# First feed-forward block fed with inputs that are not yet normalised

## The chip, the core and the metric

The kernel runs on one core of a Trainium2 chip. The metric is the device time of one launch in microseconds (us); lower is better. The engines are named as in the profile: PE is TensorE's matmul, PEld its weight load, DVE is VectorE, ACT is ScalarE, POOL is GpSimd, SP is SyncE, whose queue loads the weights.

## What is computed

Two transformer-like blocks on 256 tokens of 1024 features, in float32. The change touches the first feed-forward network (FFN) alone, the very first thing that the kernel does:

```python
def rms_norm(x, g):
    y = xf * lax.rsqrt(jnp.mean(xf * xf, axis=-1, keepdims=True) + RMS_EPS)
    return (y * g.astype(jnp.float32)).astype(x.dtype)

def swiglu(h, w1, w3, w2):
    return (jax.nn.silu(h @ w1) * (h @ w3)) @ w2

x = x + 0.5 * swiglu(rms_norm(x, ffn1_norm[l]), ffn1_w1[l], ffn1_w3[l], ffn1_w2[l])
```

D_MODEL is 1024, D_FF is 2816. The factor r = rsqrt(mean(x^2) + eps) is one number per token; the weight g is one number per feature.

## The kernel before

Activations lie with features on the 128 partitions and the 256 tokens along the free dimension, so x is eight tiles XC[:, 0, k] of 128x256. A norm is: eight squares on ACT into NT (L1544); five adds of squares (k = 1 to 5 into NT[:, 0]) on DVE (L2050, semaphore norm_acc); three sums over partitions on PE, for NT[:, 6], NT[:, 7] and NT[:, 0] (`norm_sum`, L540); the root on ACT (STD, L1548); the reciprocal on DVE (RSTD, L2069); and `norm_spread` (L558), two matmuls that lay r out as a 128x256 tile in PSUM. `norm_rows` then scales the rows on DVE into NT (L2053), rounds them on ACT to H_HI (L1554) and takes the rest H_LO = NT - H_HI on DVE (L2061).

Every float32 product is made of three rounded ones: W_HI x H_HI, W_LO x H_HI and W_HI x H_LO. Weights come in a stream of 1 MB units of 128x2048, through three buffers RAW. For each unit ACT rounds it (`split_hi`, L418, semaphore hi_done) and DVE takes the rest (`split_lo`, L430, semaphore lo_done). The SP queue loads a buffer again once lo_done says that its last unit is split. Unit 0 alone is treated by hand: ACT rounds it in two halves (L1615, L1616), and POOL takes both halves' rest (L499); after that POOL issues the loads of the tables (L501 to L504).

The FFN has 22 tiles t of 128 hidden features. `up(t)` is one unit on PE, which holds the gate tile (w = 0) and the up tile (w = 1): 16 matmuls of 128x512 (L655) and 16 of 128x256 (L659), into PSUM banks 2(t%2) and 2(t%2)+1. `down(i)` is one unit of 48 matmuls of 128x256 on the hidden tiles 2i and 2i+1 (L436, L437, L684). PE's order is written out: up(0), up(1), up(2), down(0), up(3), then a loop of up, down, up, then up(20), down(9), up(21), down(10). `up(t)` waits for lo_done of its unit and, from t = 2 on, for hid_prod of tile t-2, which frees its banks; `down(i)` waits for hid_lo of tile 2i+1.

`hidden(t)` is what stands between them. ACT copies the low halves of the two banks (L1571, L1574); DVE adds the gate (`gate_sum`, L2109); ACT takes silu (L1576); DVE adds the up tile (L2122), multiplies (L2134, hid_prod), rounds (L2139) and takes the rest (L2141, hid_lo). For the last tile, 21, the up tile is read from PSUM (L2127, L2128, L2131). On DVE the calls stand in this order: unit 1's and unit 2's split, hidden(0), unit 3's split, hidden(1), two splits, hidden(2), a split, and so on; at the end gate_sum(21), the split of the next stage's first unit, then the rest of hidden(21). On ACT: unit 2's split, silu(0), unit 3's split, silu(1), and so on. Ahead of unit 2's split ACT loads the table of silu and uses it once, on SCZ (L1621).

## Time and profile before

| | us |
|---|---|
| median of 3 runs | 1649.91 |
| lowest, highest | 1647.41, 1651.48 |
| profiled execution, its time | 1648.0 |
| profiled execution, its span | 1646.2 |
| PE busy in the span | 1627.7 |
| DVE busy | 1115.4 |
| ACT busy | 698.3 |
| POOL busy | 23.9 |

The span runs from the first to the last instruction; all starts below are counted from its beginning. PE is busy for 99% of it, but not in its first 20 us. A row of the timeline is: start, duration, engine, line, operation, output and input, shape, count, and in brackets the idle time ahead of it and who ended it. A duration of back-to-back instructions overlaps the next one's, so the distance between two starts is the price in a row of them.

### The profile page before, as it was taken

Reading aid. Unit: us, or ns where it says so; the run is one execution under the profiler, and the core shown is the slowest. Engines: PE = TensorE matmul, PEld = TensorE weight load, DVE = VectorE, ACT = ScalarE, POOL = GpSimd, SP = SyncE. Lnnn points to the kernel's source line nnn. Section 1 sums busy time; section 2 is a strip of 40 time slices with the busy share of each in tenths; the row PEclk is TensorE's granted clock in tenths of the full one; section 3 lists DMA queues with packets and bytes.
Section 4 is the critical chain, followed back from the end, with each engine's and each line's share of the span. In section 5 each row is a group of like instructions: output and inputs, shape, how many; then the busy total and the mean of one; then the engine's idle time right before and its main releaser. Section 6 shows DMA issues by size and latency. Waiting matters only on the chain.

```text
span 1646.2 us, 30278 instructions
## 1 busy us (share of the span) xinstructions
PE 1627.7 (99%) x12552; PEld 1477.9 (90%) x12552; DVE 1115.4 (68%) x1617; ACT 698.3 (42%) x918; POOL 23.9 (1%) x41
## 2 busy tenths in 40 slices
PE   9999999999999999999999999999999999999998
PEld 7999888899999999988888887988999999999997
DVE  7666657564887766668887874967457676676665
ACT  6444456434455444421222122516354445454443
POOL 1000000000000000000000000000000000000000
PEclk9999999999999999999999999999999999999998
DMA  7555477322265545243456542233323355545551
GB/s 292 178 188 194 154 283 265 120 79 105 104 237 180 203 178 195 98 158 140 164 193 253 193 166 77 103 128 104 108 77 112 146 183 187 194 154 189 192 180 52
DMA packets 37837, 267.80 MB, mean 163 GB/s; under 512 B 4268, under 2 KB 4524, under 8 KB 5744
## 3 DMA queue, kind: packets, MB, share of 16 engines
q1 hardware_dynamic: 33552, 238.25, 40.5%
q0 software_dynamic: 4192, 28.19, 4.5%
q8 instruction: 72, 1.18, 0.3%
q14 instruction: 21, 0.17, 0.0%
HBM read 265.38 MB, written 1.05 MB: 162 GB/s over the span
## 4 chain that ended last, share of the span: by engine, by line
PE 73%; issue 23%; DVE 3%; ACT 1%; DMA 0%; POOL 0%; POOLq 0%; SPq 0%; DVEq 0%; ACTq 0%
PE PS L436 15%; PE PS L437 15%; PE PS L442 11%; PE PS L655 9%; PE PS L828 6%; PE PS L659 5%; PE PS L684 2%; PE PS L892 1%; DVE W_LO L430 1%; PE PS L540 1%; PE PS L872 1%; PE PS L874 1%; PE PS L873 1%; PE PS L1178 0%; PE PS L1353 0%
## 5 line engine op out<-in xcount | busy, mean ns | idle before, releaser
L430 DVE TENSOR_TENSOR W_LO<-RAW,W_HI 128x2048 fp32r<-128x2048 f32 x210 | 476.2, 2269 | 181.8 <-ACT W_HI L418 180.9
L418 ACT ACTIVATE W_HI<-RAW 128x2048 fp32r<-128x2048 f32 x208 | 397.6, 1913 | 362.1 <-PE PS L442 239.9
L436 PE MATMUL PS<-HS,W_HI 128*128 128x256 f32 (+1 forms) x792 | 265.3, 339 | 1.5 <-ACT G L1732 0.8
L437 PE MATMUL PS<-HS,W_LO 128*128 128x256 f32 (+1 forms) x792 | 261.5, 334 | 0.0
L655 PE MATMUL PS<-HS,W_HI 128*128 128x512 f32 x984 | 246.5, 392 | 0.7 <-DVE W_LO L430 0.7
L442 PE MATMUL PS<-HS,W_HI 128*128 128x512 f32 (+1 forms) x712 | 242.1, 340 | 0.0
L436 PE MATMUL PS<-HID_HI,W_HI 128*128 128x256 f32 (+1 forms) x720 | 220.6, 307 | 0.3 <-DVE XC L2598 0.3
L437 PE MATMUL PS<-HID_HI,W_LO 128*128 128x256 f32 (+1 forms) x720 | 220.2, 307 | 0.0
L655 PEld LDWEIGHTS PS<-HS,W_HI 128*128 128x128 f32 x984 | 177.0, 189 | 32.6 <-DVE W_LO L430 0.9
L436 PEld LDWEIGHTS PS<-HS,W_HI 128*128 128x128 f32 x792 | 150.1, 189 | 19.7 <-issue 3.3
L437 PEld LDWEIGHTS PS<-HS,W_LO 128*128 128x128 f32 x792 | 150.2, 190 | 14.9
L442 PEld LDWEIGHTS PS<-HS,W_HI 128*128 128x128 f32 x712 | 134.8, 189 | 15.0
L684 PE MATMUL PS<-HID_LO,W_HI 128*128 128x256 f32 x528 | 147.9, 283 | 0.0
L436 PEld LDWEIGHTS PS<-HID_HI,W_HI 128*128 128x128 f32 x720 | 137.5, 191 | 7.6 <-issue 0.8
L437 PEld LDWEIGHTS PS<-HID_HI,W_LO 128*128 128x128 f32 x720 | 137.5, 191 | 6.2
L659 PEld LDWEIGHTS PS<-HS,W_LO 128*128 128x128 f32 x984 | 134.2, 190 | 9.6
L659 PE MATMUL PS<-HS,W_LO 128*128 128x256 f32 x984 | 137.2, 282 | 0.0
L2152 DVE SCALAR_TENSOR_TENSOR XC<-PS,GATE,XC 128x256 f32<-128x256 f32 x160 | 68.2, 478 | 53.5 <-PE PS L442 53.3
L684 PEld LDWEIGHTS PS<-HID_LO,W_HI 128*128 128x128 f32 x528 | 100.7, 192 | 0.0
L828 PE MATMUL PS<-HS,W_HI 128*128 128x256 f32 x672 | 90.9, 285 | 0.3 <-DVE W_LO L430 0.3
L828 PEld LDWEIGHTS PS<-HS,W_HI 128*128 128x128 f32 x672 | 84.5, 192 | 5.4 <-issue 4.8
L2097 DVE SCALAR_TENSOR_TENSOR SUMS<-LATE,SCZ,SUMS 128x1024 f32<-128x1024 f32 x56 | 70.1, 1282 | 1.4
(442 smaller groups left out, 2425.6 us busy)
## 6 DMA issues: line engine op xcount, KB each, us to landing
RAW<-stream SPq DMA_DIRECT2D x225, 1024.0 KB, 4.8
LATE<-stream POOLq DMA_DIRECT2D x24, 1024.0 KB, 5.1
XC<-xin SPq DMA_DIRECT2D x2, 512.0 KB, 4.6
XC<-xin POOLq DMA_DIRECT2D x1, 1024.0 KB, 5.1
out<-NT SPq DMA_DIRECT2D x4, 256.0 KB, 2.6
CON<-consts POOLq DMA_DIRECT2D x1, 616.0 KB, 6.5
LW<-lora POOLq DMA_DIRECT2D x1, 512.0 KB, 6.7
DFT<-dft POOLq DMA_DIRECT2D x1, 266.0 KB, 2.9
```

The costliest lines, as they stand in the source:

```text
L418: nc.scalar.activation(W_HI[s % RING][:], RAW[PLACE[u]][:], ACT.Copy).then_inc(hi_done, 1)
L430: last = nc.vector.tensor_tensor(W_LO[s % RING][:, o], RAW[PLACE[u]][:, o], W_HI[s % RING][:, o].bitcast(F32), ALU.subtract)
L436: nc.tensor.matmul(acc, w_hi, x_hi, start=first, stop=False)
L437: return nc.tensor.matmul(acc, w_lo, x_hi, start=False, stop=last)
L442: return nc.tensor.matmul(acc, w_hi, x_lo, start=False, stop=last)
L540: last = nc.tensor.matmul(sums(name), tmp[:, k, tt * P:(tt + 1) * P], SQW[:, k, 2 - 2 * tt:6 - 2 * tt] if w == 4 else ONE3[:, 1 - tt:3 - t ...
L655: nc.tensor.matmul(BK8[2 * (t % 2) + w][:].rearrange("p (a n) -> p a n", a=2), W_HI[sl][:, c:c + P], HS[:, :, 0, k], start=(k == 0), stop= ...
L659: last = nc.tensor.matmul(tile(w), W_LO[sl][:, c:c + P], H_HI[:, 0, k], start=False, stop=(k == KT - 1))
L684: return nc.tensor.matmul(acc, W_HI[sl][:, c:c + P], HID_LO[:, t, 0:ROWS], start=False, stop=ends)
L828: last = nc.tensor.matmul(acc, wt[sl][:, c:c + P], x(k), start=(wt is W_HI and x is rhs_hi and k == 0), stop=(x is rhs_lo and k == kt - 1))
L2097: ins = V.scalar_tensor_tensor(out=SUMS[a][:], in0=w, scalar=SCZ[:, z:z + 1], in1=SUMS[a][:], op0=ALU.mult, op1=ALU.add)
L2152: last = V.scalar_tensor_tensor(out=XC[:, h, m], in0=BK8[4 + m % 4][:, h * ROWS:(h + 1) * ROWS], scalar=gate(h, m), in1=XC[:, h, m], op0=A ...
```

## The change

In the first FFN alone, the rows that go into PE are XC times the norm's weight n1, without the factor r. Since r is one factor per token, it commutes with the product over features, and is applied afterwards: to the summed gate tile (ahead of silu) and to the summed up tile, each by one more DVE multiply with RSF, an SBUF copy of the spread factor, which ACT makes. For tile 21 the gate's second multiply takes place on the silu tile, since the up tile stays in PSUM. The norm's own chain (squares, sums, root, reciprocal, spread) is still there, but beside the first matmuls. POOL adds the squares in place of DVE, and DVE takes the rest of unit 0 in place of POOL. In up(0), PE goes through the gate tile's half of the unit as soon as ACT has rounded it, then the other half, then W_HI x H_LO, and W_LO x H_HI last.

```diff
@@ gpsimd
-            pool.wait_ge(landed[0], 16)
-            for h in range(2):
-                pool.wait_ge((S("hi_half"), hi_done)[h], 1)
-                o = slice(h * UNIT // 2, (h + 1) * UNIT // 2)
-                last = nc.gpsimd.tensor_tensor(W_LO[0][:, o], RAW[0][:, o], W_HI[0][:, o].bitcast(F32), ALU.subtract)
-            last.then_inc(lo_done, 1)
+            for k in range(1, NORM_ADDS["na"] + 1):
+                pool.wait_ge(S("norm_sq"), k + 1)
+                if k > 1:
+                    pool.wait_ge(S("norm_acc"), k - 1)
+                nc.gpsimd.tensor_tensor(NT[:, 0], NT[:, 0], NT[:, k], ALU.add).then_inc(S("norm_acc"), 1)
+            pool.wait_ge(landed[PLACE[2]], 16)
@@ tensor, up
-                    if t == 0 and f == 0:
-                        pe.wait_ge(hi_done, 1)
+                    if t < 2 and f == 0:
+                        pe.wait_ge(hi_done if t else S("half"), t + 1)
...
+                        for w in range(2):
+                            if w:
+                                pe.wait_ge(hi_done, 1)
+                            for k in range(KT):
+                                pe.wait_ge(S("norm_hi"), k + 1)
                                 c = (w * KT + k) * P
                                 nc.tensor.matmul(tile(w), W_HI[sl][:, c:c + P], H_HI[:, 0, k], start=(k == 0), stop=False)
+                            if w == 0:
+                                norm_sum("na", 0, first=6, last_k=0)
                         for w in range(2):
                             for k in range(KT):
+                                pe.wait_ge(S("norm_h"), k + 1)
                                 c = (w * KT + k) * P
+                                nc.tensor.matmul(tile_lo(w), W_HI[sl][:, c:c + P], H_LO[:, 0, k], start=False, stop=False)
+                        norm_spread("na")
+                        for w in range(2):
+                            pe.wait_ge(lo_done if w else S("half"), 1 if w else 2)
+                            for k in range(KT):
+                                c = (w * KT + k) * P
+                                last = nc.tensor.matmul(tile(w), W_LO[sl][:, c:c + P], H_HI[:, 0, k], start=False, stop=(k == KT - 1))
+                            last.then_inc(psum_ready, 1)
+                        return
...
+                            if t == 1 and f == 0 and w == 0:
+                                wait_unit(s)
@@ tensor, start
-            for k in (6, 7, 0):
+            pe.wait_ge(S("con_in"), 16)
+            keep_clock(2, 0)
+            for k in (6, 7):
                 norm_sum("na", k, first=6, last_k=0)
-            pe.wait_ge(S("con_in"), 16)
-            keep_clock(1, 0)
-            norm_spread("na")
             keep_clock(2, 0)
@@ scalar, start
+            act.wait_ge(landed[PLACE[0]], 16)
+            A(W_HI[0][:, 0:UNIT // 2], RAW[PLACE[0]][:, 0:UNIT // 2], ACT.Copy).then_inc(S("half"), 1)
+            A(W_HI[0][:, UNIT // 2:], RAW[PLACE[0]][:, UNIT // 2:], ACT.Copy).then_inc(hi_done, 1)
             act.wait_ge(S("par_in"), 16)
             root("na")
...
-            for k in range(KT):
-                round_rows("na", 0, k)
             split_hi(act, 1)
+            act.wait_ge(S("norm_spread"), NORM["na"] + 1)
+            A(RSF[:], spread_of("na"), ACT.Copy).then_inc(S("row_scale"), 1)
@@ vector, ffn
+                def by_rms(ins, rows_, n_, j=None, j0=0):
+
+                    ins.then_inc(S("summed"), 1)
+                    dve.wait_ge(S("row_scale"), 1)
+                    dve.wait_ge(S("summed"), n_ if j is None else (j - j0) * 4 + n_)
+                    return V.tensor_tensor(rows_, rows_, RSF[:], ALU.mult)
...
                     if t == FT - 1:
+                        if f == 0:
+                            link(V.tensor_tensor(SILU[:, 1, 0:ROWS], SILU[:, 1, 0:ROWS], RSF[:], ALU.mult))
@@ vector, start
-            for k in range(1, 6):
-                add_squares("na", k)
             dve.wait_ge(S("par_in"), 16)
-            dve.wait_ge(S("con_in"), 16)
+            for k in range(KT):
+                dve.wait_ge(S(f"x_in{k // 4}"), 16)
+                V.tensor_scalar(H_HI[:, 0, k], XC[:, 0, k], par("n1", k), None, ALU.mult).then_inc(S("norm_hi"), 1)
+            for k in range(KT):
+                dve.wait_ge(S("norm_hi"), k + 1)
+                V.scalar_tensor_tensor(out=H_LO[:, 0, k], in0=XC[:, 0, k], scalar=par("n1", k), in1=H_HI[:, 0, k].bitcast(F32),
+                                       op0=ALU.mult, op1=ALU.subtract).then_inc(S("norm_h"), 1)
             reciprocal("na")
-            norm_rows("na", 0, lambda k: par("n1", k))
-            dve.wait_ge(lo_done, 1)
+            for h in range(2):
+                dve.wait_ge(hi_done if h else S("half"), 1)
+                o = slice(h * UNIT // 2, (h + 1) * UNIT // 2)
+                V.tensor_tensor(W_LO[0][:, o], RAW[PLACE[0]][:, o], W_HI[0][:, o].bitcast(F32), ALU.subtract).then_inc(lo_done if h else S("half"), 1)
             split_lo(dve, 1)
```

The other lines of the diff only renumber semaphore counts (norm_t, row_scale).

PE from its first matmul to up(1), before. PS<-WARM and PS<-CON keep the engine at work, PS<-ONE_81,NT are the sums of squares, PS<-CON,RSTD the spread; W_HI_52 and W_LO_55 are unit 0, W_HI_53 and W_LO_56 unit 1.

```order
1 L901 MATMUL PS<-WARM 128x256 x9
2 L540 MATMUL PS<-ONE_81,NT 128x2 x6
3 L552 MATMUL PS<-CON 128x256
4 L558 MATMUL PS<-CON,RSTD 128x128 x2
5 L552 MATMUL PS<-CON 128x256 x2
6 L630 MATMUL PS<-HS,W_HI_52 128x256 x16
7 L635 MATMUL PS<-HS,W_LO_55 128x256 x16
8 L647 MATMUL PS<-HS,W_HI_52 128x256 x16
9 L655 MATMUL PS<-HS,W_HI_53 128x512 x8
```

And the same stretch of PE now:

```order
1 L915 MATMUL PS<-WARM 128x256 x9
2 L552 MATMUL PS<-CON 128x256 x2
3 L540 MATMUL PS<-ONE_81,NT 128x2 x4
4 L552 MATMUL PS<-CON 128x256 x2
5 L632 MATMUL PS<-HS,W_HI_52 128x256 x8
6 L540 MATMUL PS<-ONE_81,NT 128x2 x2
7 L632 MATMUL PS<-HS,W_HI_52 128x256 x8
8 L639 MATMUL PS<-HS,W_HI_52 128x256 x16
9 L558 MATMUL PS<-CON,RSTD 128x128 x2
10 L645 MATMUL PS<-HS,W_LO_55 128x256 x16
11 L667 MATMUL PS<-HS,W_HI_53 128x512 x8
```

The last sum of squares stands behind the first eight products, and the spread behind 32 of them.

DVE from the end of its memsets to the end of hidden(0), before:

```order
8 L2050 TENSOR_TENSOR NT<-NT 128x256 x5
9 L2069 RECIPROCAL RSTD<-STD 128x2
10 L2053 SCALAR_TENSOR_TENSOR NT<-XC,PAR,PS 128x256 x8
11 L2061 TENSOR_TENSOR HS<-NT,HS 128x256 x8
12 L430 TENSOR_TENSOR W_LO_56<-RAW_50,W_HI_53 128x2048
13 L2242 TENSOR_TENSOR SQW<-PAR 128x8
14 L430 TENSOR_TENSOR W_LO_57<-RAW_51,W_HI_54 128x2048
15 L2109 TENSOR_TENSOR SILU<-PS,SILU 128x256
16 L2122 TENSOR_TENSOR PROD<-PS,PROD 128x256
17 L2134 TENSOR_TENSOR PROD<-SILU,PROD 128x256
```

And now, where HS is H_HI and H_LO:

```order
8 L2269 TENSOR_SCALAR HS<-XC,PAR 128x256 x8
9 L2272 SCALAR_TENSOR_TENSOR HS<-XC,PAR,HS 128x256 x8
10 L2084 RECIPROCAL RSTD<-STD 128x2
11 L2278 TENSOR_TENSOR W_LO_55<-RAW_49,W_HI_52 128x1024 x2
12 L430 TENSOR_TENSOR W_LO_56<-RAW_50,W_HI_53 128x2048
13 L2280 TENSOR_TENSOR SQW<-PAR 128x8
14 L430 TENSOR_TENSOR W_LO_57<-RAW_51,W_HI_54 128x2048
15 L2132 TENSOR_TENSOR SILU<-PS,SILU 128x256
16 L2125 TENSOR_TENSOR SILU<-SILU,RSF 128x256
17 L2147 TENSOR_TENSOR PROD<-PS,PROD 128x256
18 L2125 TENSOR_TENSOR PROD<-PROD,RSF 128x256
19 L2166 TENSOR_TENSOR PROD<-SILU,PROD 128x256
```

Unit 0's rest has come in between the reciprocal and unit 1's split, and two multiplies with RSF into each hidden tile.

DVE at the end of the first FFN, now, from the gate sum of tile 21 to its low half:

```order
72 L2132 TENSOR_TENSOR SILU<-PS,SILU 128x256
73 L2125 TENSOR_TENSOR SILU<-SILU,RSF 128x256
74 L430 TENSOR_TENSOR W_LO_55<-RAW_49,W_HI_52 128x2048
75 L2157 TENSOR_TENSOR SILU<-SILU,RSF 128x256
76 L2159 TENSOR_TENSOR HID_HI<-SILU,PS 128x256
77 L2160 TENSOR_TENSOR PROD<-SILU,PS 128x256
78 L2163 TENSOR_TENSOR HID_LO<-PROD,HID_HI 128x256
```

Both multiplies with RSF are new there; before, the rest stood in the same order without them.

## Rows read from the trace of the kernel before

**Rows 1.** The page's first part: engine, busy us, share, instructions.

```profile
PE 1627.7 (99%) x12552; PEld 1477.9 (90%) x12552; DVE 1115.4 (68%) x1617; ACT 698.3 (42%) x918; POOL 23.9 (1%) x41
```

**Rows 2.** The chain that ended last, 0 to 60 us: start, us, what.

```profile
9.69 0.72 PE PS L558 x4
...
20.28 2.11 PE PS L655 x8
...
30.77 0.95 PE PS L659 x8
```

**Rows 3.** The timeline of all engines, 0 to 24 us.

```profile
4.86 2.80 ACT L1544 ACTIVATE NT<-XC 128x256 f32<-128x256 f32 x8 [2.83 <-DMA XC<-xin]
...
7.50 1.47 PE L540 MATMUL PS<-ONE,NT 128*128 128x2 f32 x12 [0.20 <-ACT NT L1544]
...
9.47 1.06 ACT L1615 ACTIVATE W_HI<-RAW 128x1024 fp32r<-128x1024 f32 x1
...
10.67 4.72 POOL L499 TENSOR_TENSOR W_LO<-RAW,W_HI 128x1024 fp32r<-128x1024 f32 x2 [10.22 <-ACT W_HI L1615]
...
15.93 1.28 ACT L1621 ACT_TABLE_LOAD   x1
...
17.35 1.90 ACT L418 ACTIVATE W_HI<-RAW 128x2048 fp32r<-128x2048 f32 x1
...
20.23 2.28 DVE L430 TENSOR_TENSOR W_LO<-RAW,W_HI 128x2048 fp32r<-128x2048 f32 x1
...
23.20 1.90 ACT L418 ACTIVATE W_HI<-RAW 128x2048 fp32r<-128x2048 f32 x1
23.38 0.43 DVE L2134 TENSOR_TENSOR PROD<-SILU,PROD 128x256 f32<-128x256 f32 x1 [0.20 <-DVE PROD L2122]
23.84 0.30 DVE L2139 CAST HID_HI<-PROD 128x256 fp32r<-128x256 f32 x1
```

**Rows 4.** Loads: first PAR's (issued at 1.7), then unit 0's: issue to landing.

```profile
DMA to landing us min/median/max: 4.9/4.9/4.9
L469 SPq DMA_DIRECT2D RAW<-stream x1: 432/432/432, 2.6 to 2.6; - x1
DMA to landing us min/median/max: 6.8/6.8/6.8
```

**Rows 5.** Three lines' own views: ns min/median/max, first and last start.

```profile
L2061 DVE TENSOR_TENSOR HS<-NT,HS x8: 412/414/2100, 13.6 to 17.6; 128x256 fp32r<-128x256 f32 x8
...
L523 POOL TENSOR_TENSOR NT<-SG,MT x2: 716/718/721, 1641.4 to 1642.1; 128x256 f32<-128x256 f32 x2
...
L2324 DVE TENSOR_SCALAR KK<-RKV,PAR x4: 346/348/353, 260.6 to 261.4; 128x256 f32<-128x256 f32 x4
```

**Rows 6.** The timeline, 24 to 64 us: two low halves, two starts of down.

```profile
29.22 0.43 DVE L2141 TENSOR_TENSOR HID_LO<-PROD,HID_HI 128x256 fp32r<-128x256 f32 x1
...
31.56 0.28 PE L436 MATMUL PS<-HID_HI,W_HI 128*128 128x256 f32 x1
...
45.05 0.43 DVE L2141 TENSOR_TENSOR HID_LO<-PROD,HID_HI 128x256 fp32r<-128x256 f32 x1
...
48.50 0.28 PE L436 MATMUL PS<-HID_HI,W_HI 128*128 128x256 f32 x1
```

**Rows 7.** The timeline of DVE, then of PE, end of the first FFN.

```profile
193.19 0.42 DVE L2109 TENSOR_TENSOR SILU<-PS,SILU 128x256 f32<-128x256 f32 x1 [2.45 <-ACT SILU L1571]
193.53 2.28 DVE L430 TENSOR_TENSOR W_LO<-RAW,W_HI 128x2048 fp32r<-128x2048 f32 x1
195.73 0.41 DVE L2127 TENSOR_TENSOR HID_HI<-SILU,PS 128x256 fp32r<-128x256 f32 x1
...
196.84 0.28 PE L436 MATMUL PS<-HID_HI,W_HI 128*128 128x256 f32 x1
```

**Rows 8.** Stretches: engines' busy us, granted clock (PEclk), DMA share.

```profile
10.00:12.00 2.00, 1.34 (x9) 0.92 (x8) 1.56 (x4) 2.00 (x5) 1.33 (x1) 1.00 1.03 434
...
1640.00:1646.00 6.00, 0.94 (x5) 0.65 (x4) 2.44 (x6) 0.38 (x1) 1.41 (x2) 0.50 0.49 175
```

More of the change, by code:

```diff
@@ L625, in up @@
                     if t == 0 and f == 0:
-                        for k in range(KT):
-                            pe.wait_ge(S("norm_hi"), KT * NORM_H[h_name] + k + 1)
-                            for w in range(2):
+                        for w in range(2):
[3 more added lines that the diff above has]
+                                pe.wait_ge(S("norm_hi"), k + 1)
                                 c = (w * KT + k) * P
                                 nc.tensor.matmul(tile(w), W_HI[sl][:, c:c + P], H_HI[:, 0, k], start=(k == 0), stop=False)
-                        wait_unit(s, j, j0)
+                            if w == 0:
+                                norm_sum("na", 0, first=6, last_k=0)
                         for w in range(2):
                             for k in range(KT):
+                                pe.wait_ge(S("norm_h"), k + 1)
                                 c = (w * KT + k) * P
-                                nc.tensor.matmul(tile(w), W_LO[sl][:, c:c + P], H_HI[:, 0, k], start=False, stop=(k == KT - 1))
-                    elif t == 0:
+                                nc.tensor.matmul(tile_lo(w), W_HI[sl][:, c:c + P], H_LO[:, 0, k], start=False, stop=False)
[7 more added lines that the diff above has]
+                        return
+                    if t == 0:
                         for k in range(KT):
@@ L1611, in _ @@
                 square("na", 0, k, f"x_in{k // 4}", 16)
+            act.wait_ge(landed[PLACE[0]], 16)
+            A(W_HI[0][:, 0:UNIT // 2], RAW[PLACE[0]][:, 0:UNIT // 2], ACT.Copy).then_inc(S("half"), 1)
+            A(W_HI[0][:, UNIT // 2:], RAW[PLACE[0]][:, UNIT // 2:], ACT.Copy).then_inc(hi_done, 1)
             act.wait_ge(S("par_in"), 16)
             root("na")
-            act.wait_ge(landed[PLACE[0]], 16)
-            A(W_HI[0][:, 0:UNIT // 2], RAW[PLACE[0]][:, 0:UNIT // 2], ACT.Copy).then_inc(S("hi_half"), 1)
-            A(W_HI[0][:, UNIT // 2:], RAW[PLACE[0]][:, UNIT // 2:], ACT.Copy).then_inc(hi_done, 1)
-            for k in range(KT):
-                round_rows("na", 0, k)
             split_hi(act, 1)
+            act.wait_ge(S("norm_spread"), NORM["na"] + 1)
+            A(RSF[:], spread_of("na"), ACT.Copy).then_inc(S("row_scale"), 1)
             act.wait_ge(S("set_up"), 2)
@@ L2052, in scale @@
             def scale(name, half, k, gain, dst, sem="norm_t", cols_=None):
-                V.scalar_tensor_tensor(out=dst[:, k], in0=XC[:, half, k], scalar=gain(k), in1=(spread_of(name) if cols_ is None else cols_),
-                                       op0=ALU.mult, op1=ALU.mult).then_inc(S(sem), 1)
+                ins = V.scalar_tensor_tensor(out=dst[:, k], in0=XC[:, half, k], scalar=gain(k), in1=(spread_of(name) if cols_ is None else cols_),
+                                             op0=ALU.mult, op1=ALU.mult)
+                if sem is not None:
+                    ins.then_inc(S(sem), 1)
             def rest(name, half, k, shift=None, tmp=NT):
```

26 lines of the change are left out of this document (17 added, 9 removed).

## The prediction

> **What bounds the kernel now.** I read the page's first part first: PE is busy for 1627.7 of 1646.2 us [rows 1], so only the 18.5 us in which it is idle can be won, and only a change that starts PE's work earlier moves the end. The chain that ended last shows where: until 20.28 it runs over the norm, DMA and DVE, and from 20.28 over PE's matmuls without a gap [rows 2]. So the kernel's time is the moment at which PE gets into its unbroken run, plus whatever stops it later. I take down(0)'s first matmul, 31.56 [rows 6], as the mark: everything behind it shifts with it, since the FFN behind it is PE's own, and the later waits of PE are for engines that themselves wait for PE.
>
> **What starts earlier.** Before, x waited for the factor r: root, reciprocal, spread, scaling, rounding. Unit 0 landed at 2.6 + 6.8 = 9.4 [rows 4], and ACT rounded its first half from 9.47 to 10.53 [rows 3]. That load is the same after, so PE's first product cannot start before some 10.6. From there PE's own work to up(1) is 48 products of 0.12 (eight in 0.95 [rows 2]) = 5.8, one norm_sum (1.47 for three = 0.5 [rows 3]) and the spread, 0.7 [rows 2]: 7.0. So up(1) could start at 17.6 in place of 20.28 [rows 2]: 2.7 us, which is the most that the change can bring at its front.
>
> **DVE's front, without a hold.** PAR lands at 1.7 + 4.9 = 6.6 [rows 4]. Eight TENSOR_SCALARs have starts 0.27 apart (0.8 for three steps [rows 5]): 2.2 us. Eight multiply-subtracts with two tensor inputs: an addition of two tensors has starts 0.34 apart [rows 7], and the third operand, as in the old scaling L2053, makes it 0.40: 3.2. That ends at 12.1. The root needs the last sum of squares, which PE reaches at 11.6 and ends at 12.1, so the reciprocal is through at 12.8. The halves of unit 0's rest are 1.1 each (2.20 for a whole unit [rows 7]): 15.0, and unit 1's split ends at 17.3. PE is never held up there.
>
> **DVE's front, with POOL beside it.** POOL's five adds take 0.72 each [rows 5], about 0.85 with their chained waits, from 5.65 (the second square, ACT begins at 4.86 [rows 3]) to 9.9. One row says what may come of that: of the eight subtractions of L2061 one took 2.10 where the others took 0.41; it started at 13.58 while POOL's second operation ran, and ended at 15.68, 0.3 after POOL's end at 15.39 [rows 3, 5]. Both of its inputs are in SBUF. The scalings L2053 beside POOL's first one, with one input in PSUM, were not held. So a DVE operation with two SBUF inputs is held for as long as POOL's runs. The new multiply-subtracts have two such inputs; the TENSOR_SCALARs have one tensor input, and their start distance, 0.27 against 0.34 for a sum of two tensors [rows 7], says that they run in a faster mode. No row shows such an operation beside POOL. Its bounds are no hold (nothing) and a hold for each add (POOL 0.72, DVE 0.28, in turns: the adds end at 10.3 and DVE has then done three of its sixteen). I take the second, by the nearest row, the held one. Then the other five TENSOR_SCALARs end at 11.6 and the eight others at 14.8; PE waits for each of them, and has W_HI x H_LO done at 16.0, the spread at 16.7, W_LO x H_HI at 18.6: up(1) starts 1.7 earlier than before, not 2.7.
>
> The Trainium skill (page "GPSIMD Engine Reference", Key points) says that GpSimd shares its SBUF interfaces with VectorE and contends with instructions in a 2-port mode or with two SBUF inputs. The held subtraction agrees for two inputs; for the single-input mode no row shows it. By this rule the held case above is what comes; without it the unheld one.
>
> **What takes the place of the wait.** down(0) needs hid_lo of tile 1, and that chain runs over ACT and DVE: unit 2 rounded, its rest, hidden(0), unit 3 rounded, its rest, hidden(1). Before, it ended at 29.22 + 0.43 = 29.65, 1.9 ahead of down(0) [rows 6]. It hung on ACT, which had unit 2 rounded from 17.35 behind the table load at 15.93 [rows 3]. Now the table load stands behind the RSF copy (0.35, as each of the eight squares [rows 3]), and that behind the spread on PE. Held: spread 16.7, copy, 1.42 for table and SCZ, unit 2 rounded from 18.5 to 20.4, its rest from 20.45 instead of 20.23: 0.2 later [rows 3]. Unheld: spread 15.6, rounding 17.45 to 19.35, rest from 19.4: 0.8 earlier.
>
> **What the two multiplies cost.** An operation that needs the one ahead costs 0.45 (23.38 to 23.84 [rows 3]); with a free one between it is 0.34. So hidden(0) gives silu, and with it unit 3, 0.45 later, and hidden(1) takes 0.9 longer. hid_lo(1) is then at 29.65 + 0.2 + 0.45 + 0.9 = 31.2 held, 29.65 - 0.8 + 0.45 + 0.6 to 0.9 = about 30.0 unheld. PE would be there at 18.6 + 11.3 = 29.9, or 17.6 + 11.3 = 28.9 (two ups, 20.28 to 31.56). So PE waits for hid_lo either way, and down(0) starts at about 31.3 (gain 0.3) held, at 30.0 (gain 1.5) unheld. Up to 1.4 of PE's lead is given back at this one wait.
>
> **The loop.** 44 more multiplies are on DVE in the FFN. For down(1) hid_lo(3) was there at 45.48 and PE came at 48.50 [rows 6]: 3.0 us of cover against 0.9, so these cost nothing. Without that cover each would cost 0.9 per pass.
>
> **The end of the FFN.** Tile 21's gate sum gets its multiply (0.45), unit 33's split follows it, and then a further linked multiply (0.45) before HID_HI. HID_HI ended at 195.73 + 0.41 = 196.14; PE wants it at 196.84 [rows 7]. Now it is 0.9 to 1.0 later: 197.1. PE waits 0.3. HID_LO is there by 198.0, when PE wants it at 198.06. Behind it the norm of the next stage hangs on PE. Other edits cost nothing: POOL's table loads are issued within a microsecond of before, and nobody waits for them before the stage behind the FFN; the SP queue gets units 3 to 5 within 0.4 of before, or earlier.
>
> **The sum**, against the profiled execution (span 1646.2, time 1648.0, 1.9 below the median of the runs): -0.3 + 0.3 = 0.0 held; -1.5 + 0.3 = -1.2 unheld. By the rule of the page the sum is the first, without it the second.
>
> **The rivals.** *Unheld*, 1.2 faster: 1648.7. For it: DVE takes no hold with one SBUF input and one in PSUM; against it, the faster mode of the single-input form. *DVE keeps POOL out*, slower: POOL's adds get no turn while DVE's sixteen operations stand back to back. From 6.65 to 12.3 POOL waits with three or four adds left, which end at 15.7; PE stands at the last sum of squares, behind its first eight products, the root comes at 16.4, the spread at 19.7, unit 2's rounding at 21.5 and its rest at 23.4 in place of 20.23. hid_lo(1) is at 29.65 + 3.2 + 1.35 = 34.2, down(0) 2.6 later than before, and with the 0.3 at the end the kernel is 2.9 slower: 1652.8. It decides as soon as POOL's fifth add ends behind 12.5. Against it: in the one row, DVE was the side that waited, and POOL's two operations took 2.38 each whatever DVE did. *The clock falls*: PE now idles from 9.4 to 10.6, ahead of its first product. The granted clock was 1.00 (2.4 GHz) in the stretch where PE was busy for 1.34 of 2 us, and 0.50 (1.2 GHz) in the last six, where it was busy for 0.94 [rows 8]. At 1.2 GHz up(0)'s 48 products take 5.8 more, of which the hidden-tile chain covers little: 4 to 5 slower, 1654.5. *It doesn't do what it says*: PE's lead is lost to some other wait in the loop that shrinks DVE's slack; 0.9 a pass would be nine, but the cover of 3.0 speaks against it.
>
> **How the numbers follow.** Held 0.45, unheld 0.3, DVE keeps POOL out 0.15, the clock 0.05, a loss in the loop 0.05. The likeliest is held, 1649.9 on the runs' median. The range takes in the unheld case and the slow one, each with the runs' own spread of two us around the median on the side of the gain: 1646.2 to 1653.0. A measurement of this kernel can tell about 0.3%, 5 us, from no change. No case but the last two comes near that: faster 0.03, same 0.91, slower 0.06.
>
> **What the profile after would show.** PE's first product at 10.6 and up(1)'s first 128x512 at 18.6 (held), 17.6 (unheld), 21.6 (POOL kept out). The durations of the eight TENSOR_SCALARs: three or more near 0.7 to 1.0 if held. POOL's five adds ended by 10.3. PE's wait ahead of down(0) ended by DVE's HID_LO, 0.5 to 1.5 long, and down(0) at 31.3. A wait of 0.3 ahead of the second half of down(10)'s first tiles. In the loop no PE wait at all. The prediction is wrong if PE waits in the loop, if down(0) starts below 29.5 or above 32.5, or if the granted clock falls below 1.00 in the first 30 us.

## The result and the profile after

| | before | after |
|---|---|---|
| median of 13 runs each, taken in turns on one chip | 1650.06 | 1654.07 |
| lowest, highest | 1647.41, 1651.89 | 1650.68, 1655.51 |
| profiled execution: time, span | 1648.0, 1646.2 | 1653.78, 1651.1 |
| mean granted clock of the profiled span | 0.997 | 0.994 |

The ratio is 1.0021, with a 95% interval of 1.0014 to 1.0029: the kernel became 4 us slower. That is inside the 0.3% that the prediction called no change, but 1.1 above the upper end of its range (1653.0), and 4.2 above the forecast of 1649.9.

The front of the program did start earlier. The timeline of the kernel after, 4 to 25 us (start, us, engine, line, operation, and in brackets the idle time ahead and who ended it); the rows of before that answer to it are [rows 2, 3]:

```profile
5.74 4.70 POOL L499 TENSOR_TENSOR NT<-NT 128x256 f32<-128x256 f32 x5 [5.28 <-ACT NT L1557]
6.50 4.08 DVE L2269 TENSOR_SCALAR HS<-XC,PAR 128x256 fp32r<-128x256 f32 x8 [4.56 <-DMA PAR<-params]
...
10.51 3.24 DVE L2272 SCALAR_TENSOR_TENSOR HS<-XC,PAR,HS 128x256 fp32r<-128x256 f32 x8
...
10.52 1.30 PE L632 MATMUL PS<-HS,W_HI 128*128 128x256 f32 x8
...
14.57 0.74 POOL L501 DMA_DIRECT2D CON<-consts  x1 [4.14 <-DMA RAW<-stream]
...
15.62 0.39 ACT L1632 ACTIVATE RSF<-PS 128x256 f32<-128x256 f32 x1 [1.28 <-PE PS L558]
...
16.02 1.28 ACT L1634 ACT_TABLE_LOAD   x1
...
16.36 0.55 POOL L504 DMA_DIRECT2D MOD<-bada  x1
...
17.33 2.00 PE L667 MATMUL PS<-HS,W_HI 128*128 128x512 f32 x8
...
17.44 1.90 ACT L418 ACTIVATE W_HI<-RAW 128x2048 fp32r<-128x2048 f32 x1
...
24.00 2.06 PE L667 MATMUL PS<-HS,W_HI 128*128 128x512 f32 x8 [0.92 <-DVE PROD L2166]
...
24.50 1.92 ACT L418 ACTIVATE W_HI<-RAW 128x2048 fp32r<-128x2048 f32 x1 [1.51 <-DMA RAW<-stream]
```

up(1) (the first row of L667) stands at 17.33, where before had it at 20.28 [rows 2]: PE is 2.95 us ahead. The last row is the one that matters. Unit 3's rounding on ACT waits 1.51 us for its load. Before, it started at 23.20 and waited for no load [rows 3]. The load itself, from its issue (the start is given to 0.1 us) to its landing, in the kernel after and then in the one before:

```profile
L469 SPq DMA_DIRECT2D RAW<-stream x1: 348/348/348, 16.3 to 16.3; - x1
...
DMA to landing us min/median/max: 8.2/8.2/8.2
```

```profile
L469 SPq DMA_DIRECT2D RAW<-stream x1: 348/348/348, 15.6 to 15.6; - x1
...
DMA to landing us min/median/max: 5.5/5.5/5.5
```

Further down in the kernel after, the end of hidden(1)'s chain and PE behind it:

```profile
31.57 0.43 DVE L2173 TENSOR_TENSOR HID_LO<-PROD,HID_HI 128x256 fp32r<-128x256 f32 x1
...
32.14 0.35 PE L436 MATMUL PS<-HID_HI,W_HI 128*128 128x256 f32 x1 [2.33 <-DVE HID_LO L2173]
```

down(0), the mark of the prediction, starts at 32.14, before at 31.56 [rows 6]: 0.58 later, although PE had led by 2.95 at up(1). PE stood 0.92 ahead of up(2) and 2.33 ahead of down(0), of which before had neither. The waits of PE between 24 and 200 us are these three (what waited for what: us in total, times, longest):

```profile
PE PS L436 <- DVE HID_LO L2173: 2.3, 1, 2.3
PE PS L667 <- DVE PROD L2166: 0.9, 1, 0.9
PE PS L436 <- DVE HID_HI L2159: 0.5, 1, 0.5
```

The loop has none, as before. At the end of the FFN the third wait stands (timeline after; the rows of before are [rows 7]):

```profile
194.13 0.42 DVE L2132 TENSOR_TENSOR SILU<-PS,SILU 128x256 f32<-128x256 f32 x1 [2.05 <-ACT SILU L1584]
...
197.21 0.42 DVE L2157 TENSOR_TENSOR SILU<-SILU,RSF 128x256 f32<-128x256 f32 x1
...
197.66 0.42 DVE L2159 TENSOR_TENSOR HID_HI<-SILU,PS 128x256 fp32r<-128x256 f32 x1
...
198.14 0.38 PE L436 MATMUL PS<-HID_HI,W_HI 128*128 128x256 f32 x1 [0.50 <-DVE HID_HI L2159]
```

PE's matmul stood at 196.84 before, so it is 1.30 late: 0.64 came with it from the front (the second down's first matmul stands at 49.14, before at 48.50) and 0.66 is new here. Behind it the norm of the next stage makes 2.8 us more. Its rows after, and then before (L540 sums the squares, in eight matmuls and then in four, L558 is the spread, L825 and L811 the same first product of the next stage):

```profile
204.02 1.06 PE L540 MATMUL PS<-ONE,NT 128*128 128x2 f32 x8 [1.31 <-DVE NT L2063]
...
208.14 1.23 PE L558 MATMUL PS<-CON,RSTD 128*128 128x128 f32 x4
...
215.35 0.88 PE L825 MATMUL PS<-HS,W_HI 128*128 128x256 f32 x6
```

```profile
202.62 1.05 PE L540 MATMUL PS<-ONE,NT 128*128 128x2 f32 x8 [1.31 <-DVE NT L2050]
...
205.47 0.71 PE L558 MATMUL PS<-CON,RSTD 128*128 128x128 f32 x4
...
211.20 2.08 PE L811 MATMUL PS<-HS,W_HI 128*128 128x256 f32 x16
```

The first sums are 1.40 late, the product 4.15. Between them stand no new instructions, but the same ones take longer: 1.01 against 0.61 for the last four matmuls of the sums, 1.23 against 0.71 for the spread. The view by stretches says why: the stretch, its length, busy us of PE, PEld, DVE, ACT and POOL with their instructions, the granted clock, DMA share, GB/s. After, then before:

```profile
200.00:205.00 5.00, 3.69 (x31) 3.49 (x29) 4.75 (x15) 2.89 (x8) 0.00 (x0) 0.99 0.30 125
205.00:210.00 5.00, 4.75 (x21) 2.27 (x24) 2.84 (x5) 0.62 (x3) 0.00 (x0) 0.50 0.16 33
```

```profile
200.00:205.00 5.00, 3.44 (x31) 2.76 (x30) 4.59 (x13) 2.35 (x6) 0.00 (x0) 1.00 0.00 0
205.00:210.00 5.00, 4.88 (x43) 3.42 (x36) 4.95 (x12) 3.16 (x8) 0.00 (x0) 1.00 0.55 192
```

The clock is 0.50 (1.2 GHz) from 205 to 210 after and 1.00 (2.4 GHz) before. Note that PE is not more idle from 200 to 205 after (3.69 us busy) than before (3.44). Another 0.75 us of the two spans' difference (4.9) lies behind this stage, where the profile of the kernel after has a second fall (0.66 from 440 to 445) and the one of before has none. So this pair of profiles shows a loss of 2.8 us at 205, but not that the change made it. The experiments had to find that out.

### The profile page after: what moved, and what is told of

The parts are those of the page before. It is cut to its first block, busy times and chain, and to the rows that moved or that the text cites. A ratio compares the mean times of both kernels' runs of the same rounds, so it can differ in the third digit from the quotient of the medians.

```text
span 1651.1 us, 30361 instructions
## 1 busy us (share of the span) xinstructions
PE 1632.0 (99%) x12554; PEld 1481.4 (90%) x12554; DVE 1133.0 (69%) x1658; ACT 695.2 (42%) x911; POOL 23.4 (1%) x44
## 4 chain that ended last, share of the span: by engine, by line
PE 73%; issue 23%; DVE 3%; DMA 1%; ACT 1%; POOL 0%; SPq 0%; POOLq 0%; DVEq 0%; ACTq 0%
PE PS L436 15%; PE PS L437 15%; PE PS L442 12%; PE PS L667 9%; PE PS L842 6%; PE PS L673 5%; PE PS L698 2%; PE PS L906 1%; PE PS L886 1%; PE PS L888 1%; PE PS L887 1%; PE PS L540 1%; DMA RAW<-stream 0%; PE PS L1191 0%; PE PS L1366 0%
## 5 line engine op out<-in xcount | busy, mean ns | idle before, releaser
L667 PE MATMUL PS<-HS,W_HI 128*128 128x512 f32 x984 | 246.4, 392 | 0.9 <-DVE PROD L2166 0.9
L667 PEld LDWEIGHTS PS<-HS,W_HI 128*128 128x128 f32 x984 | 177.0, 189 | 32.7 <-issue 1.1
```

Source lines behind the costliest of these rows:

```text
L667: nc.tensor.matmul(BK8[2 * (t % 2) + w][:].rearrange("p (a n) -> p a n", a=2), W_HI[sl][:, c:c + P], HS[:, :, 0, k], start=(k == 0), stop= ...
```

## The experiments

Each kernel was timed in turns with the kernel before; the ratio is to that one, in brackets its 95% interval. The mean clock is that over all executions of the kernel, each of which has its own. "Half clock" is worked out from it, as the mean over executions of 2 x (1 - clock) x span, the time that would have to be spent at 0.50. In every profile the last 5.6 to 9.8 us of the span are at 0.50 (those of before are in part in [rows 8]), and belong to it. A mean over 10 to 13 executions of one kernel is uncertain by 0.9 to 1.9 us of half clock (its standard error).

| kernel | median us | ratio | median span | mean clock | half clock us |
|---|---|---|---|---|---|
| before, again | 1650.03 | 0.9999 [0.9990, 1.0008] | 1648.2 | 0.9954 | 15.3 |
| after | 1654.07 | 1.0021 [1.0014, 1.0029] | 1652.0 | 0.9940 | 19.8 |
| after, again | 1653.7 | 1.0020 [1.0010, 1.0029] | 1651.7 | 0.9939 | 20.2 |
| tables late | 1650.5 | 1.0001 [0.9991, 1.0010] | 1648.5 | 0.9953 | 15.5 |
| split first | 1652.24 | 1.0009 [0.9999, 1.0018] | 1650.0 | 0.9950 | 16.5 |
| filler at the norm | 1652.76 | 1.0014 [1.0004, 1.0024] | 1649.8 | 0.9951 | 16.2 |
| no multiplies | 1651.87 | 1.0010 [1.0001, 1.0020] | 1649.8 | 0.9945 | 18.1 |
| tables late, split first | 1650.26 | 1.0000 [0.9991, 1.0009] | 1647.3 | 0.9951 | 16.2 |
| adds on DVE | 1653.12 | 1.0014 [1.0003, 1.0025] | 1651.3 | 0.9946 | 17.8 |
| filler in the front | 1651.34 | 1.0010 [1.0001, 1.0019] | 1649.3 | 0.9959 | 13.5 |
| table of silu first | 1647.88 | 0.9987 [0.9978, 0.9996] | 1645.9 | 0.9959 | 13.5 |
| table first, fillers | 1648.07 | 0.9983 [0.9974, 0.9992] | 1646.1 | 0.9960 | 13.2 |

The theory at the start: unit 3's load came late because POOL's four table loads, 1.3 MB, now stand ahead of it, and the rest of the loss is the clock's fall at 205, which hangs on the new wait ahead of it. The rivals: the fall belongs to the norm there and has nothing to do with the change, and the front's loss is the multiplies'.

### Tables late

```diff
-            pool.wait_ge(landed[PLACE[2]], 16)
+            pool.wait_ge(landed[PLACE[5]], 32)
```

> The changed kernel, but POOL issues the four table loads only when unit 5 has landed, so that they no longer share the DMA engines with unit 3's load. Theory (load): in the changed kernel unit 3 was issued at 16.3 behind the tables and landed at 24.5, 8.2 us later against 5.5 before, and held ACT for 1.5 us; now it lands by 21.8, ACT rounds it from 22.9, and down(0)'s first matmul is at 30.4 instead of 32.0: 1.6 us less. Rival (multiplies): the hidden-tile chain of DVE decides alone; down(0) stays at 32 and the time does not move.

Its load of unit 3, and its timeline:

```profile
L469 SPq DMA_DIRECT2D RAW<-stream x1: 348/348/348, 16.3 to 16.3; - x1
...
DMA to landing us min/median/max: 5.3/5.3/5.3
```

```profile
22.98 1.90 ACT L418 ACTIVATE W_HI<-RAW 128x2048 fp32r<-128x2048 f32 x1
...
30.60 0.36 PE L436 MATMUL PS<-HID_HI,W_HI 128*128 128x256 f32 x1 [0.71 <-DVE HID_LO L2173]
```

Issued at the same 16.3, unit 3 landed 5.3 us later instead of 8.2, ACT didn't wait for it, and down(0) started 1.54 earlier than in the kernel after, 0.96 earlier than before. This part of the theory stands. All thirteen profiles of this study agree: unit 3's load takes 7.7 to 8.9 us in the seven where the tables are issued from 14.6 to 16.6, and 5.2 to 5.8 in the other six, where they come later or, as before, start 0.3 ahead of it (CON at 15.33). POOL had been busy with unit 0's rest until 15.3 in the kernel before [rows 3], and that had kept all but the first of its tables off the DMA engines when unit 3's load was issued. In the kernel after, only the wait for unit 2's landing, which the change put there, holds them back, to 14.57; and unit 3's load is issued 0.7 later than before, because DVE is through with unit 0's rest at 16.08, where POOL was at 15.39. The Trainium skill (page "Trainium Kernel Development and Optimization", Key Constraints) says that transfers issued from the queues of SP, ACT and POOL all run on the same 16 engines and interleave; 8.2 against 5.3 us agrees with it.

The kernel became 3.6 us faster than the one after (1650.5 against 1654.07; 3.3 by the ratios, whose intervals at most touch), more than the 1.54 of the shift; its half clock is 4.3 us shorter. The wait of 0.5 at the end of the FFN stayed. So this one wait of POOL's recovers nearly the whole loss, and a part of what it recovers is the clock's.

### Split first

```diff
+                    if i == 10 and f == 0:
+                        split_lo(dve, s + 4, j, j0)
                     if i == 10 and halves == 1:
                         gate_sum(2 * i + 1)
-                    split_lo(dve, s + 4, j, j0)
+                    if not (i == 10 and f == 0):
+                        split_lo(dve, s + 4, j, j0)
```

> The changed kernel, but at the end of the first FFN DVE takes unit 33's rest ahead of tile 21's gate sum and not behind it. PE's wait of 0.5 us for HID_HI goes, 0.5 us less. Theory A (the granted clock's fall to 0.50 at 205 hangs on that wait): the clock is 1.00 from 190 to 220 and the kernel is 3.3 us faster. Theory B (it hangs on the low activity of the norm behind it, which stays as it was): the fall is still there in most executions, and only 0.5 us go.

Its waits of PE between 24 and 205 us:

```profile
PE PS L436 <- DVE HID_LO L2173: 2.2, 1, 2.2
PE PS L540 <- DVE NT L2063: 1.3, 1, 1.3
PE PS L667 <- DVE PROD L2166: 0.9, 1, 0.9
...
```

The wait for HID_HI is gone, and the fall behind it is not. Two stretches of this kernel:

```profile
205.00:210.00 5.00, 4.74 (x27) 2.44 (x30) 3.59 (x6) 0.91 (x3) 0.00 (x0) 0.70 0.13 20
...
32.00:36.00 4.00, 3.96 (x22) 3.99 (x23) 4.00 (x2) 2.10 (x3) 0.00 (x0) 0.61 0.42 127
```

So the fall doesn't hang on that wait: the theory's second half was wrong. But there is a second fall, at 32 us, right behind the wait for HID_LO (2.2), where the profile of the kernel after has none. The time is 1.8 below that of the kernel after (1652.24), where Theory B forecast 0.5; the intervals of the ratios overlap, so the surplus is not established.

### Filler at the norm

```diff
+                    if i == 10 and f == 0:
+                        keep_clock(2, 0)
                     if i == 10 and then != "nd":
                         norm(then)
```

> The changed kernel with 1 us of filler matmuls (two of 128x256 in float32) on PE in the 1.3 us gap between down(10)'s last matmul and the norm's first sum; nothing else. Theory B (the clock falls for want of activity around the norm): the clock is 1.00 through 200 to 220, the mean granted clock rises from 0.993 to 0.995 or more, and the kernel is 2.8 us faster. Theory A (it hangs on the wait ahead of down(10)'s second half) or chance: no gain, the fall is still there.

The profile shows a clock of 0.93 from 205 to 210 and 0.73 from 210 to 215, and a fall at 32 of its own (0.50 from 32 to 36). The time is 1.3 below that of the kernel after, with intervals that overlap, against 2.8 forecast; the mean clock rose to 0.9951, as forecast. This one settles little. From the norm's first sum to the next stage's first product PE takes 9.98 us here; the second profile of the kernel after, without a filler, takes 10.00.

### No multiplies

```diff
-                        ins = by_rms(ins, to, 2 * t + 1, j, j0)
+                        pass
...
-                            ins = by_rms(ins, up_, 2 * t + 2, j, j0)
+                            pass
...
-                            link(V.tensor_tensor(SILU[:, 1, 0:ROWS], SILU[:, 1, 0:ROWS], RSF[:], ALU.mult))
```

> The changed kernel without the multiplies by the norm's factor (this part of the computation is left out: the first FFN's hidden tiles lack the factor). Theory (load decides the front): hid_lo of tile 1 comes 0.9 us earlier, since unit 3's landing at 24.5 still holds the chain ahead of it; down(0) at 31.1, and PE's wait at tile 21 goes: 1.4 us less in all. Rival (multiplies decide): 1.35 us at down(0) and more in the loop, over 2 us in all.

```profile
24.43 1.92 ACT L418 ACTIVATE W_HI<-RAW 128x2048 fp32r<-128x2048 f32 x1 [1.92 <-DMA RAW<-stream]
...
30.45 0.43 DVE L2172 TENSOR_TENSOR HID_LO<-PROD,HID_HI 128x256 fp32r<-128x256 f32 x1
...
31.03 0.36 PE L436 MATMUL PS<-HID_HI,W_HI 128*128 128x256 f32 x1 [2.05 <-DVE HID_LO L2172]
```

HID_LO is 1.12 earlier than in the kernel after, which is what the multiplies of hidden(1) cost, and the wait of 0.92 ahead of up(2), which those of hidden(0) had caused, is gone. The wait for the load got longer by what they had hidden of it (1.92 against 1.51). down(0) is 1.11 earlier without the multiplies and 1.54 earlier without the tables ahead of the load: both hold it up, and the load is the larger cause. Each of the two kernels has down(0) earlier than before (by 0.53 and 0.96), so it takes both together to lose the front.

The time fell by 2.2 (1651.87; 1.8 by the ratios). The theory said 1.4 and the rival over 2, so by the time alone the rival would have won; down(0) at 31.03 is the theory's 31.1. The rows give 1.11 there and 0.75 at the end of the FFN (from down(0) to the norm's first sum 171.13 against 171.88), and the rest may be the clock's: half clock is 1.7 us shorter, which is within its uncertainty.

### Before again and after again

Both kernels unchanged, to see what belongs to the execution and what to the kernel.

> The kernel before, unchanged, with the span and the mean granted clock of each execution, which its first times lacked. Theory (the clock): its executions carry fewer stretches at half clock than the changed kernel's; their mean clocks lie at 0.995 to 0.997, and those at 0.997 have spans of about 1646.5, so the changed kernel at equal clock (two executions of 1647.7 and 1648.7 at 0.997) is only 1 to 2 us slower. Rival (the clock is the same in both): its clocks lie at 0.993 to 0.994 as in the changed kernel, and the 4 us are all waits.

> The changed kernel, unchanged, beside the kernel before on one chip. Clock theory: mean clock 0.993 to 0.995 in most executions, span at 0.997 near 1648, median 3.5 to 4.5 us above the kernel before. Rival (the first comparison caught an unlucky mix of executions): median within 2.5 us of the kernel before.

The second profile of the kernel before has a fall at 205 too:

```profile
205.00:210.00 5.00, 5.00 (x27) 2.08 (x23) 3.56 (x8) 1.99 (x6) 0.00 (x0) 0.66 0.46 152
```

So the fall at 205 is found in both kernels; the 2.8 us that the first two profiles show there are for a good part the luck of which execution was profiled. The second profile of the kernel after has one at 32, behind a wait of 3.05:

```profile
32.89 0.55 PE L436 MATMUL PS<-HID_HI,W_HI 128*128 128x256 f32 x1 [3.05 <-DVE HID_LO L2173]
...
32.00:36.00 4.00, 3.11 (x14) 3.14 (x15) 3.97 (x4) 2.94 (x4) 0.00 (x0) 0.50 0.44 184
```

Neither profile of the kernel before has a fall in its first 200 us. Of the thirteen profiles six have a wait of 2.04 us or more ahead of down(0), and four of these fall at 32 (after again 3.05, filler at the norm 2.73, split first 2.20, adds on DVE 2.04); two don't (after 2.33, no multiplies 2.05). Of the seven with a wait of at most 0.85 or none, none falls there. Over all executions half clock is 15.3 us before and 19.8 and 20.2 after (15.6 in the 90 executions of before that were timed beside the experiments). That difference, 4.7, or 4.3 with these 90 and a standard error of 0.9, is the kernel's, and the clock theory's forecasts held in the main: after again is 3.8 above before in its session.

What it costs can be read from the executions of one kernel: those of before ran from a span of 1645.6 at a clock of 0.997 to 1649.6 at 0.994, 4.0 us for 9.9 us more of half clock, about 0.4 for each (a straight line through all executions gives 0.32 to 0.37). So 4.7 us of it make 1.5 to 1.9. At equal clock, 0.997, before has spans of 1645.6 and 1646.0, and after 1647.7 and 1648.7: 2.4 more. The two together are 3.9 to 4.3, against 4.0 measured. Of the 2.4, rows show 1.40 (the start of the norm's sums, 204.02 against 202.62). The other 1.0 has no row; since clocks are given to 0.001, which is 3.3 us of half clock or about 1.3 us of span, it may be nothing. So the split of the 4 us into waits and clock is good to about 1 us.

The rows of the second pair make a check. The norm's first sum starts at 203.01 in before again and at 207.31 in after again (L540). That is 4.30 of the 4.4 by which these two spans differ (1652.4 against 1648.0). down(0) is 0.94 late (32.89 against 31.95). From there to the norm's first sum PE takes 171.06 in both profiles of before, 171.88 in the first one of after and 174.42 here: 0.82 for the end of the FFN, and 2.54 for the fall at 32. Both then take 10.00 to the next product, and the rest of the span is the same to 0.1. So this pair lost 1.76 by waits and 2.54 by the clock at 32; the first pair 1.40 by waits and nothing at 32. In the other three profiles with that fall it cost 1.5, 1.5 and 2.6 by the same rows. Averaged over the six profiles with the long wait it is about 1.4 (an estimate from six executions), so the clock at 32 is the larger part of the kernel's 1.5 to 1.9, and whether the change also makes the falls at 205 and 440 more frequent is open.

### Both mended

The edits of tables late and split first together.

> The changed kernel with both edits: table loads behind unit 5's landing, and unit 33's rest ahead of tile 21's gate sum. If the two are independent: down(0) at 30.5, no wait at tile 21, so 2.1 us less than the changed kernel at equal clock, a span near 1646.0 at 0.997, that is 0.3 to 0.5 us below the kernel before; the median 0 to 1 us below it. Rival: what is won in front is lost at PE's low-activity stretch at 200 to 210, by more stretches at half clock, and the median is above the kernel before by 0.5 us or more.

1650.26: equal to before, 3.8 below the kernel after. The two edits alone gave 3.6 and 1.8, so they don't add up; the second brings no more than the measurement's width once the first is there. By the rows it brings 0.72 (from down(0) to the norm's first sum 171.15, with tables late alone 171.87). At a clock of 0.997 its one execution has a span of 1645.3, 0.5 below before's, while down(0) is 0.96 earlier.

### Adds on DVE

```diff
-            for k in range(1, NORM_ADDS["na"] + 1):
-                pool.wait_ge(S("norm_sq"), k + 1)
-                if k > 1:
-                    pool.wait_ge(S("norm_acc"), k - 1)
-                nc.gpsimd.tensor_tensor(NT[:, 0], NT[:, 0], NT[:, k], ALU.add).then_inc(S("norm_acc"), 1)
...
+            for k in range(1, 6):
+                add_squares("na", k)
```

> The changed kernel, but the five adds of squares are back on DVE, ahead of the eight TENSOR_SCALARs, and POOL computes nothing. Theory (hold): with POOL idle the TENSOR_SCALARs have starts 0.3 apart and take 2.2 us together, not 4.1; they begin 2.4 later (8.2 and not 6.5 at the latest 8.9), end at 10.6 as before, and the rest of the front and the time do not move: moving the adds to POOL brought nothing. Rival (no hold, the TENSOR_SCALAR to the rounded type is itself that slow): they take 4.1 here too, end at 12.5, up(1) is 1 us later and the kernel 0.5 to 1 us slower.

```profile
5.73 2.55 DVE L2058 TENSOR_TENSOR NT<-NT 128x256 f32<-128x256 f32 x5 [3.79 <-ACT NT L1552]
8.20 2.19 DVE L2266 TENSOR_SCALAR HS<-XC,PAR 128x256 fp32r<-128x256 f32 x8
10.29 3.25 DVE L2269 SCALAR_TENSOR_TENSOR HS<-XC,PAR,HS 128x256 fp32r<-128x256 f32 x8
```

Eight TENSOR_SCALARs take 2.19 with POOL idle and 4.08 beside POOL's adds. Each one's own duration, min/median/max in ns, is in the line's view, after and then here:

```profile
L2269 DVE TENSOR_SCALAR HS<-XC,PAR x8: 341/582/819, 6.5 to 9.8; 128x256 fp32r<-128x256 f32 x8
```

```profile
L2266 DVE TENSOR_SCALAR HS<-XC,PAR x8: 348/348/349, 8.2 to 10.0; 128x256 fp32r<-128x256 f32 x8
```

The hold is real, and it eats the whole gain of the adds' move: with all five adds on DVE the multiply-subtracts start 0.22 earlier (10.29 against 10.51), and up(1) at 17.32 against 17.33. The median, 1653.12, is the kernel after's within the intervals. The rule of the Trainium skill that the prediction named (page "GPSIMD Engine Reference", Key points: contention with a 2-port mode) fits 4.08 against 2.19 as far as the contention goes; that these TENSOR_SCALARs ran in such a mode no run here shows. And the hold is not a full one: five adds alone would take 3.6 us (718 ns each [rows 5]) and the eight TENSOR_SCALARs 2.19, 5.8 together, but both were through within 4.84 (5.74 to 10.58).

### Filler in the front

```diff
                 up(2, s0 + 2)
+                if f == 0:
+                    keep_clock(4, 5)
                 down(0, s0 + 3)
```

> The changed kernel with 2 us of filler matmuls (four of 128x256 in float32) on PE ahead of down(0), inside its new wait of 2.3 to 3.0 us. Theory (the granted clock falls at 32 us in some executions because PE stands still there): no execution loses the clock at 32 any more, the mean granted clock over all executions rises from 0.9940 to 0.995 and the median falls by 1 to 1.7 us, the intercept at equal clock staying. Rival (the extra half-clock time has nothing to do with that wait): mean clock 0.994, median within 0.5 us of the changed kernel's.

```profile
32.00:36.00 4.00, 3.51 (x29) 3.54 (x30) 4.00 (x3) 2.54 (x4) 0.00 (x0) 1.00 0.50 164
```

The filler does no work that the output needs, and down(0) starts no earlier in the profile (32.49). Still the kernel is 2.4 to 2.7 faster than the one after (1651.34 against 1653.7 and 1654.07; 1.6 to 1.8 by the ratios, whose intervals overlap at their ends), and half clock fell from 20 to 13.5 us, by more than its uncertainty. PE's wait for HID_LO is 0.85 in place of 2.33. So PE's wait ahead of down(0) costs by its length and by the clock behind it; that no execution at all falls at 32 any more, one profile can't show. Half clock is below that of the kernel before (15.3), too, which one place at 32 us doesn't explain. It may be chance (the uncertainty of each is over 1 us, and this profile still has the falls at 205, 0.70, and 440, 0.75).

### Table of silu first

The edits of both mended, and on ACT the copy RSF, which waits for PE's spread, goes behind the table load and unit 2's rounding:

```diff
                 split_hi(act, s0 + 2)
+                if f == 0:
+                    act.wait_ge(S("norm_spread"), NORM["na"] + 1)
+                    A(RSF[:], spread_of("na"), ACT.Copy).then_inc(S("row_scale"), 1)
                 silu(0, m0 + 1)
...
             split_hi(act, 1)
-            act.wait_ge(S("norm_spread"), NORM["na"] + 1)
-            A(RSF[:], spread_of("na"), ACT.Copy).then_inc(S("row_scale"), 1)
```

> The kernel with both edits (tables late, unit 33's rest first), and on ACT the silu table, SCZ and unit 2's rounding ahead of the copy of the factor, so that they no longer wait for the spread at 15.6. Theory (the hidden chain's start on ACT sets down(0)): unit 2 is rounded from 15.7 and not 17.5, DVE takes its rest from 18.3, PE's wait of 0.9 ahead of up(2) goes, down(0) starts at 29.5 instead of 30.5: 1 us less, a span near 1644.2 at clock 0.997, median 1.5 to 2 us below the kernel before. Rival: unit 3's load (lands 21.8) holds ACT next, and only 0.3 us come.

```profile
15.65 1.90 ACT L418 ACTIVATE W_HI<-RAW 128x2048 fp32r<-128x2048 f32 x1
...
29.31 0.36 PE L436 MATMUL PS<-HID_HI,W_HI 128*128 128x256 f32 x1 [0.69 <-DVE HID_LO L2174]
```

This one beats both kernels: 1647.88, 2.4 below the 1650.29 of before in the same session, and 6.2 below the kernel after. In the kernel after, ACT had waited 1.28 us for the spread and copied it before it loaded the table; now the table load starts at 14.23 in place of 16.02, unit 2 is rounded from 15.65 in place of 17.44, and down(0) starts 2.25 ahead of before and 2.83 ahead of after. The norm's first sum stands at 200.47, 2.15 ahead of before, so that most of the 2.4 is in the rows.

### Table first, with fillers

The kernel above, with `keep_clock(1, 5)` ahead of down(0) and `keep_clock(2, 0)` ahead of the norm.

> The same with 0.5 us of filler ahead of down(0) and 1 us ahead of the norm's sums behind the first FFN. If idle PE time at these two places is what costs clock: mean clock at 0.9960 or more, median 0.5 to 1 us below the kernel without fillers. Rival (fillers delay the norm's sums a little and change no clock): the same median or up to 0.5 us more.

1648.07 against 1647.88: no difference, as the rival said. Where PE waits 0.69 in place of 2.3 to 3.0, a filler has nothing left to save, and the filler ahead of the norm didn't take away the fall there (0.83 from 200 to 210).

## Why the prediction was wrong

- **The mark held only for the waits.** The loop has no PE wait, and the first 33 us, the end of the FFN and the clock make the 4 us, within the 1 us left open above. But down(0) moved by 0.58 and 0.94 in the two pairs of profiles, and the time by 4: "everything behind it shifts with it" left out what PE's clock does behind a wait. Of its signs of being wrong the first profile after shows none (down(0) at 32.14, under 32.5), the second shows one (32.89); the clock fell behind the 30 us that it watched, at 32.
- **The step that failed** is in the part on the end of the FFN: "POOL's table loads are issued within a microsecond of before, and nobody waits for them". The first half is true: issued at 14.57 to 16.36 after, 15.33 to 17.13 before. The second counts those who wait for the tables, and not those who share the DMA engines with them. Unit 3's load was issued at 16.3 after and 15.6 before, so before only the first table had been issued ahead of it, by 0.3 us, and now it stands behind nearly all of the 1.3 MB: 8.2 us in place of 5.5, landed at 24.5 in place of 21.1. That cost 1.5 at down(0), as tables late showed. Without it down(0) came at 30.60 (tables late), between the forecasts held, 31.3, and unheld, 30.0; with it at 32.14. The front's own gain was thus 0.96, where the forecast had 0.3, and this hid a part of what the load cost. "The SP queue gets units 3 to 5 within 0.4 of before" failed too: unit 3's load was issued 0.7 later. In the text's own held case DVE would have ended unit 0's rest at about 17.2, 1.8 later than POOL did before, so the two statements didn't fit together; tables late has the same 0.7 and lost nothing by it. Moving the tables alone gave back 3.3 to 3.6 of the 4.0, more than the 1.5, since with PE's wait at 0.71 the clock's share went too.
- **The clock rival had the right effect at the wrong place, and too small a chance (0.05).** It looked for PE's idle time ahead of up(0), where the clock stayed at 1.00. The wait that the same text forecast ahead of down(0) was never weighed as a place for a fall. It came out at 2.3 to 3.05 instead of 1.4, and the clock falls behind it in part of the executions. The forecast put this term at nothing; it is 1.5 to 1.9 of the 4.0. The rival's own price for low clock, 5.8 us more for 48 products, took each for twice as long; by the rows three of down(0)'s products take 0.64 at 0.50 and 0.36 at 1.00, which makes 4.5. The end of the FFN, which the first pair of profiles pointed to, has its fall in both kernels.
- **End of the FFN**: forecast 0.3, measured 0.50 by the wait and 0.66 by the start. The term was the chain on DVE, 0.9 to 1.0 against a cover of 0.7 (196.14 to 196.84). By the rows HID_HI starts 1.93 later (197.66 against 195.73): 0.94 at the gate sum (194.13 against 193.19), 0.54 for the multiply ahead of the split and 0.45 for the one behind it. PE itself is 0.64 late there, so the chain grew by 1.29 against it, and 0.3 of that is a later start of the gate sum, which no step had.
- **Held or unheld**: held was right for the TENSOR_SCALARs (4.08 for eight; 582 ns the median, 2.2 unheld). But POOL's adds and DVE's operations shared better than "DVE has then done three of its sixteen": by 10.6 (6.50 and 4.08) all eight were through. The eight multiply-subtracts ended at 13.75, not 14.8, and up(1) came at 17.33, forecast 18.6 held and 17.6 unheld. The bound "a hold for each add" took a row of an operation with two SBUF inputs (2.10 against 0.41 [rows 5]) for one with a single tensor input. Here 819 ns was the longest.
- **Right**: PE's first product at 10.52 (10.6), POOL's adds over at 10.44 (10.3), the link price of 0.45 for each dependent multiply, the cover in the loop, that PE would wait for hid_lo and give its lead back there. The wait of 0.9 ahead of up(2), for hid_prod, was not foreseen; by the rows it took nothing of its own, as down(0)'s wait would have been longer without it; no run took it out alone.
- **DVE keeps POOL out** did not happen: POOL's adds took 852 ns each at the median, alone 718 [rows 5].
- **The range** ended at 1653.0. It held the 2.9 of a rival that did not come; with the load (1.5) and the clock (1.5 to 1.9) beside the forecast its middle would have been 1652.9 to 1653.3, near what was measured.

## What to carry to other kernels

A transfer that nobody waits for still has a price: ask of each queue what is issued in the same few microseconds, and which load that somebody does wait for then stands behind it; an engine that is relieved of work can issue its DMAs earlier, and one that is given work can free a buffer later. When a change makes one engine early, look for the chain that now ends last before counting the gain, and fill that chain's own waits (here ACT's for the spread) first. A wait of two or three microseconds on TensorE can cost more than its length, so compare mean clocks over many executions of both kernels, and several profiles of each, since a single pair of profiles can blame the wrong place.
